# One 256-column product for the next tile's channel mean and this tile's variance, with GpSimd's channel sums moved to the head of its tile

## The chip, the cores and the metric

The kernel runs on one core of a Trainium2 chip. Its time is the device time of one execution in microseconds (us), as the median of several runs. The engines are TensorE (PE, with its weight loads as PEld), VectorE (DVE), ScalarE (ACT), GpSimd (POOL) and SyncE (SP, which issues most of the DMAs). Each works through its own instructions in order, and they meet through semaphores.

## What is computed

One layer of a streaming encoder on 2048 positions of 1024 channels, in float32. A combined projection gives queries, keys, values and the input `u` of a convolution branch. Attention looks at a window of 128 keys and has a sink term per head. The branch is a gated causal convolution with 31 taps, then a layer norm over its 512 channels and swish. Both halves go through a shared output projection, a residual and a layer norm. A gated MLP with a 3-tap convolution and a second residual and layer norm follow. The part that matters here is the norm of the branch:

```python
def layer_norm(x, g, b):
    mu = jnp.mean(xf, axis=-1, keepdims=True)
    var = jnp.mean(jnp.square(xf - mu), axis=-1, keepdims=True)
    y = (xf - mu) * lax.rsqrt(var + LN_EPS)
    return (y * g + b)

def conformer_conv(u, conv_w, conv_b, ln_g, ln_b):
    a, gate = jnp.split(u, 2, axis=-1)
    h = causal_depthwise_conv(a * jax.nn.sigmoid(gate), conv_w, conv_b)
    return jax.nn.silu(layer_norm(h, ln_g, ln_b))
```

## The kernel before, in words

There are four stages: projection with the convolution (until about 317 us of the profiled span), mixing (until about 600 us), up projection and down projection. The change lies in the mixing stage, which works on 16 tiles of 128 positions. It is written out by hand as a software pipeline: in each pass of a loop every engine runs a `body(q, p, c, n, m)` on five tiles at once, where n is the tile whose scores and softmax are made, m = n + 1 the next, and c = n - 1, p = n - 2, q = n - 3 the ones before. A first few passes and the last ones are unrolled around a loop of two tiles per turn (`bodies`). The order of the calls in `body` is the order of the engine's queue.

The branch lies transposed: 512 channels as 4 groups of 128 partitions, 128 positions along the free dimension (`conv_in`). A sum over the channels needs two steps. GpSimd adds the four groups, pairwise and then to one (`sum_conv`, L1428 to L1434, into `conv_sum`; `sum_squares`, L1436 to L1442, into `square_sum`). TensorE then multiplies with a matrix of 1/512 (`ones`), which sums over the partitions and leaves the mean on all of them (`means`, L2373; `variance`, L2391). Mean and variance are written to the same 128 columns of the PSUM bank `aux`, so `means(m)` waits until the variance of n has been used up (`cn_ok`). The next columns hold `ct` and `cr`, steps of the inverse root, and `sink_ps`.

One tile's way through the norm is this. TensorE gives the mean; VectorE subtracts it (`centre`, L2141, into `cc`); ScalarE squares (L1708); GpSimd sums the squares (L1439, L1442); TensorE gives the variance (L2394); ScalarE takes the logarithm and the exponential (`conv_root`, L1723, L1725), which makes an inverse root `cy`; VectorE refines it (`conv_norm`, L2213, L2215, L2217) and scales `cc` (L2220). ScalarE's gate chain (L1731, L1739) and VectorE's swish follow, and they feed the output projection of the next pass (L2413).

The queues around the change, in one pass:

- GpSimd: `cosines(m)` (L1387), `sum_squares(n)`, `sum_conv(m)`, `rotate(m)` (L1415, L1421, L1424, which wait for VectorE's sine products L2135 and L2136), `affine(p)` (L1446, L1448, which wait for VectorE's row norm L2177). The first affine step belongs to tile 0 and runs in the pass of n = 2; the last belongs to tile 12.
- TensorE: `values(c)` (L2470), `scores(n)` (L2386), output products of c (L2413), `turn_values(n)` (L2402), more output products, `variance(n)`, `turn_rows(q)` (L2456), output products of groups 4 and 5, transposes of the probabilities (L2462), output products of groups 6 and 7 (whose end is `y_ps`), `means(m)`.
- VectorE: residual (L2118), gate and attention parts of c, two softmax shifts with `centre(n)` between them, swish, softmax sums (L2205) and reciprocals (L2207), `conv_norm(n)`, row statistics (L2148), sine products, row norm (L117 to L121, L2177).
- ScalarE: casts, exponentials, squares, `conv_root(n)`, probabilities (L1718), copies of the turned rows (L1781), gate inputs, copies of the turned probabilities (L1786), gate chain.

The code of the functions that the diff touches:

Of the kernel before, what the change touches and what calls it, by code (L numbers as in the profile page):

```python
# [793 lines left out]
def phase_rest(nc, block, head, trig_scr, par, con, w_o, ln1_g, ln1_b, h_scr, qkv_scr, conv_scr, h1T_scr, w_tiles, act_scr, w_down, ln_g, ln_b, h1_scr, low_scr, out):  # L794
    ctx, mix, up = ExitStack(), ExitStack(), ExitStack()
    with ctx:
# [32 lines left out]
        conv_pair, square_pair = msb("m_conv_pair", [P, 2, P]), msb("m_square_pair", [P, 2, P])  # L829
        conv_sum, square_sum = msb("m_conv_sum", [P, P]), msb("m_square_sum", [P, P])  # L830
        cy, cln = msb("m_cy", [P, P]), msb("m_cln", [P, P])
# [16 lines left out]
        tps = mps("m_tps", [P, 2 * BLK])  # L848
        mean = var = aux[:, 0:P]
        ct, cr = aux[:, P:2 * P], aux[:, 2 * P:3 * P]  # L850
        sink_ps = aux[:, 3 * P:3 * P + NKV * GROUPS].rearrange("p (g a) -> p g a", g=NKV)
# [268 lines left out]
        def closing(p):  # L1120
            return isinstance(p.t, int) and p.t >= NT - 3

        @block.sync
# [207 lines left out]
        def _(pool):  # L1331
# [96 lines left out]
            def sum_conv(n):  # L1428
                pool.wait_ge(vc_ld[n.slot], n.nth * 32 + 32)
                after(pool, conv_sum_ok, n.t)  # L1430
                nc.gpsimd.tensor_tensor(conv_pair[:, :, :], conv_in[:, n.slot, 0:2, :], conv_in[:, n.slot, 2:4, :], ALU.add).then_inc(conv_pair_ok, 1)
                pool.wait_ge(conv_pair_ok, n.t + 1)
                after(pool, mean_ps, n.t)
                nc.gpsimd.tensor_tensor(conv_sum[:], conv_pair[:, 0, :], conv_pair[:, 1, :], ALU.add).then_inc(conv_sum_ok, 1)  # L1434

            def sum_squares(n):  # L1436
                pool.wait_ge(square_ok, n.t + 1)
                after(pool, square_sum_ok, n.t)
                nc.gpsimd.tensor_tensor(square_pair[:, :, :], squares[:, 0:2, :], squares[:, 2:4, :], ALU.add).then_inc(square_pair_ok, 1)  # L1439
                pool.wait_ge(square_pair_ok, n.t + 1)  # L1440
                after(pool, var_ps, n.t)
                nc.gpsimd.tensor_tensor(square_sum[:], square_pair[:, 0, :], square_pair[:, 1, :], ALU.add).then_inc(square_sum_ok, 1)  # L1442

# [6 lines left out]
            def body(q, p, c, n, m):  # L1450
                if m is not None:
                    cosines(m)
                if n is not None:
                    sum_squares(n)
                if m is not None:
                    sum_conv(m)
                    rotate(m)
                if p is not None and not closing(p):
                    affine(p)
                    if isinstance(p.t, int) and p.t == 0:  # L1460
                        head.clear()
                elif c is not None and p is None:
                    pool.wait_ge(trig_rest_ld, 16 * 8)
                    pool.wait_ge(mrow_ld, 32)
# [441 lines left out]
        def _(dve):  # L1906
# [231 lines left out]
            def centre(n):  # L2138
                dve.wait_ge(mean_ps, n.t + 1)
                after(dve, cact_seq, 4 * n.t - 2)  # L2140
                nc.vector.tensor_tensor(cc[:, :, :], conv_in[:, n.slot, :, :], each(mean, CT), ALU.subtract).then_inc(centre_ok, 1)  # L2141
# [45 lines left out]
            def soft_shift(n, g):  # L2187
# [5 lines left out]
                dve.wait_ge(soft_seq, soft_at(n, g, 1))  # L2193
                dve.wait_ge(mean_ps, n.t + 1)
                nc.vector.scalar_tensor_tensor(out=peak[:, g, :], in0=top[:, g, :], scalar=SCALE, in1=sink_ps[:, g, :], op0=ALU.mult,
# [13 lines left out]
            def conv_norm(n):  # L2209
                seq = Count(cn_seq, dve)  # L2210
                seq.base = n.t * 3
                dve.wait_ge(cy_ok, n.t + 1)
                seq.inc(nc.vector.scalar_tensor_tensor(out=ct, in0=var, scalar=EPS, in1=cy[:], op0=ALU.add, op1=ALU.mult))  # L2213
                seq.wait()
                seq.inc(nc.vector.scalar_tensor_tensor(out=ct, in0=ct, scalar=-0.5, in1=cy[:], op0=ALU.mult, op1=ALU.mult))  # L2215
                seq.wait()
                seq.inc(nc.vector.scalar_tensor_tensor(out=cr, in0=ct, scalar=1.5, in1=cy[:], op0=ALU.add, op1=ALU.mult))  # L2217
                seq.wait()
                assert seq.n == 3
                nc.vector.tensor_tensor(cc[:, :, :], cc[:, :, :], each(cr, CT), ALU.mult).then_inc(cn_ok, 1)  # L2220

# [125 lines left out]
        def _(pe):  # L2347
# [25 lines left out]
            def means(n):  # L2373
                pe.wait_ge(conv_sum_ok, n.t + 1)
                after(pe, cn_ok, n.t)
                nc.tensor.matmul(mean, ones[:], conv_sum[:], start=True, stop=True).then_inc(mean_ps, 1)

# [13 lines left out]
            def variance(n):  # L2391
                pe.wait_ge(square_sum_ok, n.t + 1)
                pe.wait_ge(shift_ok, NKV * n.t + NKV)
                nc.tensor.matmul(var, ones[:], square_sum[:], start=True, stop=True).then_inc(var_ps, 1)  # L2394

# [78 lines left out]
            def body(q, p, c, n, m):  # L2474
# [4 lines left out]
                else:  # L2479
# [8 lines left out]
                    if c is not None:  # L2488
                        project_rest(c)
                if n is not None:  # L2490
                    variance(n)
# [7 lines left out]
                if c is not None:  # L2499
                    project_conv(c, (6, 7))  # L2500
                if m is not None:
                    means(m)

# [365 lines left out]
```

## Time and profile before

| | us |
|---|---|
| median of 3 runs | 1906.34 |
| lowest and highest run | 1905.53, 1906.53 |
| span of the profiled execution | 1901.2 |
| median less span | 5.1 |
| TensorE busy in the span | 1862.5 (98%) |
| VectorE, ScalarE, GpSimd busy | 1537.4, 950.8, 909.4 |

The span runs from the first to the last instruction of one profiled execution; what lies around it in a run is not shown by the profile. Busy times are sums over an engine's instructions, and they say nothing of which engine set the pace. In a timeline a row is: start in us, length in us, engine, line, operation, output <- inputs, shape, count, and in square brackets the idle time of that engine ahead of it with what ended it. One product of float32 operands shows as two matmul records and two weight loads. Ends of matmuls are modelled.

### The profile page before, as it was taken

The numbers are of one execution on the slowest core, as the hardware profiler recorded it, in microseconds if no ns is written. First come the engines' busy times: TensorE is split into PE (matmuls) and PEld (weight loads), VectorE is DVE, ScalarE is ACT, GpSimd is POOL, SyncE is SP. The second block draws the span as 40 slices with busy tenths as digits, with TensorE's granted clock in tenths as the row PEclk, the third lists the DMA queues.
The fourth block names the chain that finished last, engine by engine and source line by source line (L and its number), as shares of the span: only waits on it lengthen the run. The fifth ranks groups of instructions, "written<-read, shape, count | busy, mean of one in ns | idle before, by whom it ended". The sixth has DMA issues, their size and how long they took to land.

```text
span 1901.2 us, 26980 instructions
## 1 busy us (share of the span) xinstructions
PE 1862.5 (98%) x8632; PEld 1527.4 (80%) x8632; DVE 1537.4 (81%) x1938; ACT 950.8 (50%) x1483; POOL 909.4 (48%) x666
## 2 busy tenths in 40 slices
PE   8999999999999899999999999999999999999998
PEld 7888888777777688888888778888888788888886
DVE  8877993799998888988988988878788755676787
ACT  3455662777778545444445444444444532232453
POOL 2169994266675354444545544444443865430000
PEclk9999999999999899999999999999999999999999
DMA  7411123644563433332334332323234654587554
GB/s 280 172 44 44 44 83 122 207 136 143 170 207 111 144 110 124 136 111 105 122 138 170 112 115 101 114 90 109 101 112 145 198 157 140 167 264 246 183 170 144
DMA packets 201828, 265.80 MB, mean 140 GB/s; under 512 B 12320, under 2 KB 131360, under 8 KB 200480
## 3 DMA queue, kind: packets, MB, share of 16 engines
q1 hardware_dynamic: 188096, 229.32, 36.5%
q10 hardware_dynamic: 13664, 35.66, 5.0%
q8 instruction: 32, 0.52, 0.1%
q14 instruction: 36, 0.29, 0.0%
HBM read 177.18 MB, written 87.75 MB: 139 GB/s over the span
## 4 chain that ended last, share of the span: by engine, by line
PE 57%; issue 17%; DVE 11%; POOL 7%; ACT 4%; DMA 2%; SPq 1%; POOLq 0%; DVEq 0%; ACTq 0%
PE d_y L2793 20%; PE u_mm L2364 20%; PE a_mm L250 15%; POOL u_w_sum L1338 1%; ACT m_ce L1739 1%; POOL u_w_sum L1336 1%; PE m_y L2413 1%; POOL u_s L1356 1%; POOL u_s L1359 1%; ACT m_tps L1731 1%; DVE m_stat L2148 1%; POOL u_s L1353 1%; DVE u_w_lo L1909 1%; DVE m_top L2192 1%; DVE m_den L2205 1%
## 5 line engine op out<-in xcount | busy, mean ns | idle before, releaser
L2364 PE MATMUL u_mm<-u_forms,u_w_hi 128*128 128x512 f32 x2464 | 763.1, 391 | 11.0 <-issue 4.6
L2364 PEld LDWEIGHTS u_mm<-u_forms,u_w_hi 128*128 128x128 f32 x2464 | 462.9, 188 | 112.8 <-issue 10.9
L2364 PE MATMUL u_mm<-u_forms,u_w_lo 128*128 128x512 f32 x1232 | 480.8, 390 | 0.0
L2793 PE MATMUL d_y<-d_wd,d_a_hi 128*128 128x512 f32 x1232 | 379.6, 389 | 1.4 <-DVE d_a_lo L1033 1.3
L250 PE MATMUL a_mm<-a_hT,a_w_hi 128*128 128x512 f32 x896 | 278.2, 392 | 1.9 <-DVE a_hT L535 1.9
L2793 PEld LDWEIGHTS d_y<-d_wd,d_a_hi 128*128 128x128 f32 x1232 | 231.0, 188 | 50.2 <-DVE d_a_lo L1033 1.7
L2364 PEld LDWEIGHTS u_mm<-u_forms,u_w_lo 128*128 128x128 f32 x1232 | 232.1, 188 | 48.7
L2793 PE MATMUL d_y<-d_wd,d_a_lo 128*128 128x512 f32 x616 | 239.7, 389 | 0.0
L1949 DVE SCALAR_TENSOR_TENSOR u_y<-u_z,u_taps,u_y 128x1024 f32<-128x1024 f32 x176 | 222.6, 1286 | 10.4 <-DVE u_z L1963 3.1
L1336 POOL TENSOR_TENSOR u_w_sum<-u_w_raw 128x512 f32<-128x512 f32 x44 | 60.2, 1368 | 291.7 <-DMA u_w_raw<-w_up 291.6
L250 PEld LDWEIGHTS a_mm<-a_hT,a_w_hi 128*128 128x128 f32 x896 | 166.7, 188 | 37.5 <-DVE a_hT L535 3.4
L250 PE MATMUL a_mm<-a_hT,a_w_lo 128*128 128x512 f32 x448 | 174.6, 390 | 0.0
L1017 ACT CAST d_a_hi<-d_a_raw 128x1408 fp32r<-128x1408 f32 x56 | 77.0, 1375 | 184.4 <-PE d_y L2793 180.7
L1909 DVE TENSOR_TENSOR u_w_lo<-u_w_raw,u_w_hi 128x512 fp32r<-128x512 f32 x132 | 149.0, 1130 | 21.8 <-ACT u_w_hi L1522 21.7
L1909 DVE TENSOR_TENSOR u_w_lo<-u_w_sum,u_w_hi 128x512 fp32r<-128x512 f32 x176 | 146.9, 840 | 16.8 <-ACT u_w_hi L1522 14.3
L1522 ACT CAST u_w_hi<-u_w_sum 128x512 fp32r<-128x512 f32 x176 | 105.2, 620 | 110.2 <-POOL u_w_sum L1338 45.4
L2413 PE MATMUL m_y<-m_wo,m_mix_hi 128*128 128x512 f32 x512 | 141.9, 402 | 1.5 <-ACT m_mix_hi L1704 1.4
L473 POOL TENSOR_TENSOR a_gb<-a_gb,a_spare 128x512 f32<-128x512 f32 x112 | 130.2, 1212 | 24.3 <-ACT a_spare L392 24.3
L1033 DVE TENSOR_TENSOR d_a_lo<-d_a_raw,d_a_hi 128x1408 fp32r<-128x1408 f32 x56 | 102.7, 1833 | 40.3 <-ACT d_a_hi L1017 39.9
L2793 PEld LDWEIGHTS d_y<-d_wd,d_a_lo 128*128 128x128 f32 x616 | 115.6, 188 | 24.1
L1346 POOL TENSOR_TENSOR u_w_sum<-u_w_raw,u_w_sum 128x512 f32<-128x512 f32 x44 | 63.9, 1452 | 147.2 <-DVE u_w_lo L1909 147.2
L1575 ACT ACTIVATE u_gy<-u_y 128x1024 f32<-128x1024 f32 x44 | 45.2, 1028 | 168.1 <-DVE u_y L1949 168.1
(245 smaller groups left out, 2948.6 us busy)
## 6 DMA issues: line engine op xcount, KB each, us to landing
u_w_raw<-w_up SPq DMA_DIRECT2D x44, 1024.0 KB, 4.9
d_a_raw<-gated_scr SPq DMA_DIRECT2D x56, 704.0 KB, 5.1
gated_scr<-u_s SPq DMA_DIRECT2D x88, 256.0 KB, 2.0
d_wd_raw<-w_down SPq DMA_DIRECT2D x88, 256.0 KB, 5.2
gated_scr<-u_gy SPq DMA_DIRECT2D x44, 256.0 KB, 2.1
a_xs<-x SPq DMA_DIRECT2D x16, 512.0 KB, 5.6
m_h_in<-h_scr SPq DMA_DIRECT2D x16, 512.0 KB, 4.0
h_scr<-m_r SPq DMA_DIRECT2D x16, 512.0 KB, 4.8
```

Source lines behind the costliest of these rows:

```text
L250: last = nc.tensor.matmul(mm[bank][:], w[:, k, :], hT[n][:, part, k, :], start=(k == 0 and w is hi and part == HI_PART), stop=(k == KT - 1 ...
L473: nc.gpsimd.tensor_tensor(p, p, prod[:, i % 2, 0:size], ALU.add).then_inc(part_ok, 1)
L1017: nc.scalar.copy(a_hi[:, u % 2, :, :], a_raw[:, u % 2, :, :]).then_inc(ahi_ok, 1)
L1033: nc.vector.tensor_tensor(a_lo[:, u % 2, :, :], a_raw[:, u % 2, :, :], a_hi[:, u % 2, :, :].bitcast(F32), ALU.subtract).then_inc(alo_ok, 1)
L1336: nc.gpsimd.tensor_tensor(w_sum[:, 0, :, :], a21, raw_of(Q4), ALU.add).then_inc(sum_ok, 1)
L1346: nc.gpsimd.tensor_tensor(w_sum[:, 0, :, :], raw_of(Q2), w_sum[:, 1, :, :], ALU.subtract).then_inc(sum_ok, 1)
L1522: nc.scalar.copy(w_hi[:, s, :, :], left_of(s)).then_inc(whi_ok, 1)
L1909: nc.vector.tensor_tensor(w_lo[:, s, :, :], left_of(s), w_hi[:, s, :, :].bitcast(F32), ALU.subtract).then_inc(wlo_ok, 1)
L1949: v = nc.vector.scalar_tensor_tensor(out=y[:, m, :], in0=z[:, m, k:k + SPAN], scalar=tap(st, m, k), in1=y[:, m, :], op0=ALU.mult, op1=ALU.add)
L2364: last = nc.tensor.matmul(mm[BANK[s]][:], w[:, s, k, :], forms[:, POS[s], part, k, :], start=(s in FRESH and k == 0 and w is w_hi and part ...
L2413: m = nc.tensor.matmul(ym[:, at], a[:, c.slot, k, :], wo_part(part, k)[:, at], start=opens, stop=closes)
L2793: m = nc.tensor.matmul(dy[u % BANKS][:], a[:, u % 2, k, :], wd[:, ph % 2, k, part, :], start=(k == 0 and a is a_hi and part == HI_PART), s ...
```

## The change

The channel sum and the square sum become the two halves of one buffer, `sums`. In the pass of tile n TensorE no longer makes a 128-column product for the variance of n in its middle and another for the mean of n + 1 at its end. It makes one product of 256 columns in the place of the variance, whose first half is the mean of tile n + 1 and whose second half is the variance of tile n. It counts on `var_ps`; `mean_done` says which count stands for the mean of a tile. The means of tiles 0 and 1 and the variances of tiles 0 and 15 are still made by products of their own. For the one product both sums must be there, so GpSimd's `sum_conv(m)` goes from behind `sum_squares(n)` to the head of its pass, ahead of `cosines(m)`, and the product waits for `conv_sum_ok` of m as well. Before `sum_conv` overwrites its half it waits for the product that read it last. Mean and variance have 128 columns each in `aux`, `ct` the third, and the last step of the refinement writes `ct` in place.

```diff
-        conv_sum, square_sum = msb("m_conv_sum", [P, P]), msb("m_square_sum", [P, P])
+        sums = msb("m_sums", [P, 2, P])
+        conv_sum, square_sum = sums[:, 0, :], sums[:, 1, :]
...
-        mean = var = aux[:, 0:P]
-        ct, cr = aux[:, P:2 * P], aux[:, 2 * P:3 * P]
+        mean, var, ct = (aux[:, k * P:(k + 1) * P] for k in range(3))
+        moments = aux[:, 0:2 * P]
...
+        def mean_done(t):
+
+            return (mean_ps, t + 1) if isinstance(t, int) and t < 2 else (var_ps, t)
...
-                after(pool, mean_ps, n.t)
-                nc.gpsimd.tensor_tensor(conv_sum[:], conv_pair[:, 0, :], conv_pair[:, 1, :], ALU.add).then_inc(conv_sum_ok, 1)
+                if not isinstance(n.t, int) or n.t:
+                    pool.wait_ge(*mean_done(n.t - 1))
+                nc.gpsimd.tensor_tensor(conv_sum, conv_pair[:, 0, :], conv_pair[:, 1, :], ALU.add).then_inc(conv_sum_ok, 1)
...
             def body(q, p, c, n, m):
                 if m is not None:
+                    sum_conv(m)
                     cosines(m)
                 if n is not None:
                     sum_squares(n)
                 if m is not None:
-                    sum_conv(m)
                     rotate(m)
...
             def centre(n):
-                dve.wait_ge(mean_ps, n.t + 1)
+                dve.wait_ge(*mean_done(n.t))
...
-                seq.inc(nc.vector.scalar_tensor_tensor(out=cr, in0=ct, scalar=1.5, in1=cy[:], op0=ALU.add, op1=ALU.mult))
+                seq.inc(nc.vector.scalar_tensor_tensor(out=ct, in0=ct, scalar=1.5, in1=cy[:], op0=ALU.add, op1=ALU.mult))
...
+            def variance_and_mean(n, m):
+                pe.wait_ge(conv_sum_ok, m.t + 1)
+                pe.wait_ge(square_sum_ok, n.t + 1)
+                pe.wait_ge(shift_ok, NKV * n.t + NKV)
+                pe.wait_ge(cn_ok, n.t)
+                nc.tensor.matmul(moments, ones[:], sums[:, :, :].rearrange("p s t -> p (s t)"), start=True, stop=True).then_inc(var_ps, 1)
...
-                if n is not None:
+                if m is not None:
+                    variance_and_mean(n, m)
+                elif n is not None:
                     variance(n)
...
-                if m is not None:
-                    means(m)
```

## Rows read from the trace of the kernel before

**Rows 1.** Busy times in the window of the mixing stage's steady part.

```profile
core 0: us, PE busy (x) PEld busy (x) DVE busy (x) ACT busy (x) POOL busy (x), PEclk, DMA share, GB/s
386.00:575.00 189.00, 188.64 (x1094) 149.09 (x1092) 178.24 (x376) 145.25 (x338) 132.04 (x120) 1.00 0.53 164
```

**Rows 2.** Window of one tile's period, same columns.

```profile
433.30:449.47 16.17, 16.13 (x96) 12.72 (x94) 15.27 (x34) 12.51 (x30) 10.90 (x10) 1.00 0.49 145
```

**Rows 3.** GpSimd's groups, 386 to 575 us (count, busy, mean ns, idle before).

```profile
L1431 POOL TENSOR_TENSOR m_conv_pair<-m_conv_in 128x256 f32<-128x256 f32 x12 | 8.8, 731 | 0.0
```

**Rows 4.** Timeline of GpSimd through one tile.

```profile
449.56 2.38 POOL L1446 TENSOR_TENSOR m_r<-m_r,m_g 128x1024 f32<-128x1024 f32 x1 [1.14 <-DVE m_r L2177]
...
454.38 1.57 POOL L1387 TENSOR_TENSOR m_qk_cos<-m_qk_in,m_cos 128x640 f32<-128x640 f32 x1
455.91 0.73 POOL L1439 TENSOR_TENSOR m_square_pair<-m_squares 128x256 f32<-128x256 f32 x1
456.72 0.46 POOL L1442 TENSOR_TENSOR m_square_sum<-m_square_pair 128x128 f32<-128x128 f32 x1
457.15 0.72 POOL L1431 TENSOR_TENSOR m_conv_pair<-m_conv_in 128x256 f32<-128x256 f32 x1
...
458.35 0.24 POOL L1415 COPY m_kr<-m_kr 128x64 f32<-128x64 f32 x1
462.54 0.83 POOL L1421 TENSOR_TENSOR m_kr<-m_qk_cos,m_qk_sin 128x128 f32<-128x128 f32 x1 [3.95 <-DVE m_qk_sin L2135]
```

**Rows 5.** Timelines of TensorE, ScalarE and VectorE around the same tile's variance.

```profile
456.80 0.61 PE L2413 MATMUL m_y<-m_wo,m_mix_lo 128*128 128x512 f32 x2
457.32 0.48 PE L2394 MATMUL m_aux<-m_square_sum,m_ones 128*128 128x128 f32 x2
...
457.31 0.30 PEld L2394 LDWEIGHTS m_aux<-m_square_sum,m_ones 128*128 128x128 f32 x2 [0.32 <-issue]
...
457.84 0.37 ACT L1723 ACTIVATE m_cln<-m_aux,m_eps 128x128 f32<-128x128 f32 x1 [0.61 <-PE m_aux L2394]
458.24 0.31 ACT L1725 ACTIVATE m_cy<-m_cln 128x128 f32<-128x128 f32 x1
...
448.66 0.81 DVE L2177 TENSOR_SCALAR m_r<-m_r,m_mv,m_l 128x1024 f32<-128x1024 f32 x1
...
458.58 0.18 DVE L2207 RECIPROCAL m_inv<-m_den 128x4 f32<-128x4 f32 x1
458.67 0.27 DVE L2213 SCALAR_TENSOR_TENSOR m_aux<-m_aux,m_cy 128x128 f32<-128x128 f32 x1
```

**Rows 6.** TensorE's timeline where a tile starts; then two groups, 386 to 575 us.

```profile
449.01 0.39 PE L2376 MATMUL m_aux<-m_conv_sum,m_ones 128*128 128x128 f32 x2
449.32 1.08 PE L2470 MATMUL m_pv<-m_probT,m_vw 128*64 128x256 f32 x8
...
L2470 PE MATMUL m_pv<-m_probT,m_vw 128*64 128x256 f32 x88 | 11.9, 392 | 0.0
...
L2376 PE MATMUL m_aux<-m_conv_sum,m_ones 128*128 128x128 f32 x22 | 4.3, 274 | 0.0
```

**Rows 7.** GpSimd's timeline for tiles 2 and 15; chain of waits for tile 2.

```profile
371.10 1.56 POOL L1387 TENSOR_TENSOR m_qk_cos<-m_qk_in,m_cos 128x640 f32<-128x640 f32 x1 [2.44 <-PE m_score L2386]
...
584.36 0.74 POOL L1439 TENSOR_TENSOR m_square_pair<-m_squares 128x256 f32<-128x256 f32 x1 [0.60 <-ACT m_squares L1708]
...
368.56 0.22 PE m_aux L2376 x2
...
376.82 0.24 PE m_aux L2394 x2
```

**Rows 8.** Windows where TensorE stood still (columns as in rows 1); chain of waits.

```profile
341.00:345.00 4.00, 2.46 (x26) 1.84 (x26) 3.10 (x3) 3.78 (x6) 0.00 (x0) 1.00 1.00 386
...
636.00:642.00 6.00, 5.58 (x15) 3.89 (x14) 3.23 (x3) 5.21 (x8) 2.90 (x3) 0.61 0.19 57
...
635.35 5.46 PE u_mm L2364 x12
```

**Rows 9.** Chain of waits behind the mixing stage's last probabilities.

```profile
596.72 11.19 PE m_y L2413 x48
```

More of the change, by code:

```diff
@@ L1441, in sum_squares @@
                 after(pool, var_ps, n.t)
-                nc.gpsimd.tensor_tensor(square_sum[:], square_pair[:, 0, :], square_pair[:, 1, :], ALU.add).then_inc(square_sum_ok, 1)
+                nc.gpsimd.tensor_tensor(square_sum, square_pair[:, 0, :], square_pair[:, 1, :], ALU.add).then_inc(square_sum_ok, 1)
             def affine(p):
@@ L2193, in soft_shift @@
                 dve.wait_ge(soft_seq, soft_at(n, g, 1))
-                dve.wait_ge(mean_ps, n.t + 1)
+                dve.wait_ge(*mean_done(n.t))
                 nc.vector.scalar_tensor_tensor(out=peak[:, g, :], in0=top[:, g, :], scalar=SCALE, in1=sink_ps[:, g, :], op0=ALU.mult,
@@ L2216, in conv_norm @@
                 seq.wait()
-                seq.inc(nc.vector.scalar_tensor_tensor(out=cr, in0=ct, scalar=1.5, in1=cy[:], op0=ALU.add, op1=ALU.mult))
+                seq.inc(nc.vector.scalar_tensor_tensor(out=ct, in0=ct, scalar=1.5, in1=cy[:], op0=ALU.add, op1=ALU.mult))
                 seq.wait()
                 assert seq.n == 3
-                nc.vector.tensor_tensor(cc[:, :, :], cc[:, :, :], each(cr, CT), ALU.mult).then_inc(cn_ok, 1)
+                nc.vector.tensor_tensor(cc[:, :, :], cc[:, :, :], each(ct, CT), ALU.mult).then_inc(cn_ok, 1)
             def log_gate(n):
@@ L2375, in means @@
                 after(pe, cn_ok, n.t)
-                nc.tensor.matmul(mean, ones[:], conv_sum[:], start=True, stop=True).then_inc(mean_ps, 1)
+                nc.tensor.matmul(mean, ones[:], conv_sum, start=True, stop=True).then_inc(mean_ps, 1)
             def scores(n):
@@ L2393, in variance @@
                 pe.wait_ge(shift_ok, NKV * n.t + NKV)
-                nc.tensor.matmul(var, ones[:], square_sum[:], start=True, stop=True).then_inc(var_ps, 1)
+                nc.tensor.matmul(var, ones[:], square_sum, start=True, stop=True).then_inc(var_ps, 1)
+            def variance_and_mean(n, m):
[4 more added lines that the diff above has]
+                nc.tensor.matmul(moments, ones[:], sums[:, :, :].rearrange("p s t -> p (s t)"), start=True, stop=True).then_inc(var_ps, 1)
             def turn_values(n):
```

## The prediction

> **What bounds the kernel now.** I read the page first. By its busy times, in the table above, TensorE works for 98% of the span, which invites the reading that any product taken from it is time won. The windows by stage say where the change acts: in the 189 us of the mixing stage's steady part TensorE is busy for 188.64, VectorE for 178.24, GpSimd for 132.04, at full clock [rows 1]. One tile in it takes 16.17 us with TensorE busy for 16.13 and VectorE for 15.27 [rows 2]. Two engines are that full, so a busy share does not decide; the waits within one tile have to be followed.
>
> The timeline of one tile shows a ring. VectorE normalises tile n-2 (L2177) until 448.66 + 0.81 = 449.47. GpSimd starts its affine step (L1446) at 449.56, after waiting 1.14 us for it, and from there issues without a gap: L1446, L1448, the cosines at 454.38, the squares' pair at 455.91, the squares' sum at 456.72, done at 457.18 [rows 3, 4]. TensorE's weight load for the variance starts at 457.31, the product at 457.32, though its weight loads had been idle for 0.32 us: it waited for that sum [rows 5]. ScalarE waits 0.61 us for the product and starts the logarithm at 457.84 and the exponential at 458.24, which ends at 458.55. VectorE's L2213, which needs it, starts at 458.67 [rows 5]. From there VectorE runs down to the next L2177, and that releases GpSimd's next affine step. The ring is closed: its length is the period of 16.17 us [rows 2].
>
> How much play has the ring? Where an engine really waits for another here, the start follows the release by 0.03 to 0.14 us: the logarithm starts 0.04 after the product's end (457.32 + 0.48 = 457.80). L2213 could thus have started at about 458.59. It started at 458.67, right behind VectorE's own reciprocal at 458.58 [rows 5]. So the chain of waits runs along VectorE here, but the ring through GpSimd is only 0.08 us shorter. TensorE has at most about 0.05 us of play at the variance: an output product takes it 0.23 us (11.19 us for 48 [rows 9]), so the last two ahead of the variance, from 456.80 [rows 5], end their turn near 457.26, against 457.32.
>
> **The change part by part.** (a) The channel sums (L1431, L1434) move from behind the squares to ahead of the cosines, so into the ring between affine and squares. Their slot is read from start to start: pair at 457.15, next instruction behind the sum at 458.35, so 1.20 us [rows 4] (the pair alone lasts 0.73 [rows 3]). Before, they ran beside a stretch behind which GpSimd idled for 3.95 us waiting for VectorE's sine products [rows 4], so they cost nothing there; the same 1.20 us ahead of the squares is not covered, because GpSimd has no gap between 449.56 and 457.18. The cosines are delayed as well, but are only read after that idle time. The added wait in the channel sum (for the variance product of the tile before) was fulfilled most of a period earlier: nothing.
>
> (b) The variance is now the second half of a 256-column product. The trace has no such product with 128 rows of output, but has 256-column ones with 64: a record of theirs lasts 392 ns, one of the mean product's 128 columns 274 [rows 6]. Result later by 392 - 274 = 118 ns, say 0.12 us, with the start of the second pass set by the same weight load. Bounds: 0 (the result counts from the issue) to 0.3 (both passes wait in full). I take 0.12, the difference of the two nearest rows.
>
> (c) The product of the mean at the end of each tile (0.31 us, from 449.01 to 449.32 [rows 6]) disappears. That is a true saving of TensorE time, but the product stands behind `y_ps`, and the next one needs ScalarE's transposed probabilities, which come at about the same time. Once the ring is 1.2 us longer TensorE has room, and the saving is worth 0 in the steady part.
>
> (d) The mean now comes a third of a tile or more earlier. The centring on VectorE is not waiting for it in the trace: no idle time stands before it. Worth 0. The separate places of mean, variance and `ct` change only addresses.
>
> (e) Queued behind TensorE's variance wait are the row transposes, the conv products, the probability transposes and, through them, the whole next tile's start. They shift with it. Behind ScalarE's logarithm stand the probabilities and the gate inputs, behind L2213 the rest of VectorE's tile. All of them stand downstream of the same point, so they shift by one amount, not by several.
>
> Sum for one tile: 1.20 + 0.12 - 0.08 (the play) = +1.24 us, so a period of about 17.4 us. How many tiles pay? Those in which the squares follow an affine step and channel sums: n = 3 to 14, twelve, as the twelve records of L1431 in the steady part confirm [rows 3]. For the tiles before, GpSimd waits for scores ahead of the cosines (2.44 us for tile 2 [rows 7]; the two tiles before it wait in the same way), and the channel sums fit into that wait. The last tile has no channel sums ahead, and GpSimd waits 0.60 us for its squares [rows 7]. Twelve times 1.24 is 14.9 us. In tile 2 TensorE itself is the path: the chain runs through the mean product with 0.22 us, which goes, and through the variance product, which grows by 0.12 [rows 7]; -0.1 to -0.3, say -0.2. Nothing behind the stage absorbs the rest: the chain goes from ScalarE into 48 output products of TensorE [rows 9] and on into the next stage, with no load in it that started at a fixed time. Result: +14.7 us on the profiled span of 1901.2, so 1915.9 us of span. The median of the runs, 1906.34, is 5.1 above the span; I add the same, 1906.34 + 14.7 = 1921.0 us.
>
> Bounds: the play taken as 0.14 and (b) as 0 give 1.06 a tile, 12.7 - 0.6 = +12.1 us; (b) as 0.3 and no play give 1.5 a tile, +18 us. So 1918.4 to 1924.4; with 1 us for the spread of medians and another for a second-order loss, 1917 to 1926.
>
> **The rivals.** *Hidden* (time about 1906). The channel sums would be covered after all if something other than the squares' sum released the variance product. For it: the chain of waits never names GpSimd in this stage. Against it: the weight-load idle before L2394 and ScalarE's wait behind it occur in all twelve tiles. At a play of 1.3 us a tile instead of 0.08 the change would cost nothing. Here I also put the case that the diff does less than it seems to.
>
> *Faster* (1902). If TensorE's own stream sets the period, each tile gives back the 0.31 us of the mean product less at most 0.1 for the wider one: fourteen mean products in tiles 2 to 15 go, 14 x 0.31 = 4.3 us, so 1902.0. It decides as long as the squares' sum is there when TensorE gets to the variance at 457.26; it comes at 457.18 now, and 1.20 later after the change. It would take a GpSimd that starts its affine step more than a microsecond earlier, and VectorE, which releases it, has no idle time to give.
>
> *The clock falls* (about 1970). TensorE would now stand still for over 1 us in each tile. The trace shows a stand of 1.5 us between 341 and 345 us with the clock at 1.00 (2.4 GHz), and near 636 us, after stretches in which TensorE was busy for less than half, 0.61, where twelve products took 5.46 us, 0.455 each in place of 0.228 [rows 8]. If half of a tile's 48 output products ran at the lower level (1.2 GHz), that would be 24 x 0.228 = 5.5 us, less 1.2 of idle time, 4.3 a tile, 52 in all: 1921 + 52 = 1973. The steady part would keep TensorE busy for over 90%, which is far from the stretches where it fell. The Trainium skill ("TensorE: Matmul & The Clock Gate", "A second HAM failure mode: psum-queue depth-cycling") describes a kernel in which short idles between groups of matmuls, frequent enough, made the clock go up and down; by that rule the twelve new idles would do it. No row here shows it for idles that short.
>
> **How the numbers follow.** Forecast (GpSimd's sums lengthen the ring) 0.87; hidden 0.05; faster 0.05; clock 0.03. The range 1917 to 1926 holds nearly all of the first. Slower by over 0.2% (3.8 us, about what a measurement of this kernel can tell from none): 0.87 + 0.03 = 0.90. Within: 0.05. Faster: 0.05, though its 4.3 us lie near the edge.
>
> **What would show it.** Right: in the steady part GpSimd goes channel sums, cosines, squares without a gap; the squares' sum ends about 9 us after L1446 starts, not 7.6; TensorE's weight load for the moments stands idle for over 1.2 us before it; VectorE gets idle time before L2213, released by ScalarE's exponential, near 1.2 us; a period near 17.4 us; the clock at 1.00; the stages before and after as long as now. Wrong: a period of 16.2 or less (hidden, faster), L2213 without idle time, or a clock under 1.00 between 386 and 600 us. If the period grows by clearly less than 1.1 us, the play was misread; by more than 1.5, the wide product or a second wait was.

## The result: 19 us slower, and the profile after

| | before | after |
|---|---|---|
| median of the runs of one sitting | 1906.12 (4 runs) | 1925.72 (4 runs) |
| lowest and highest run | 1905.53, 1906.53 | 1924.29, 1927.84 |
| ratio, with its 95% interval | 1 | 1.0099 [1.0082, 1.0116] |
| span of the profiled execution | 1901.2 | 1926.1 |
| TensorE busy in the span | 1862.5 | 1866.5 |
| VectorE, ScalarE, GpSimd busy | 1537.4, 950.8, 909.4 | 1541.1, 950.6, 911.7 |

The median lies 4.7 us above the forecast and just inside its range. The sum behind the forecast was too small, though. Where did the time go? GpSimd's affine step is a mark that comes once per period. These are the rows of its line in both kernels (count, shortest/median/longest in ns, first to last start in us). Lines of the mixing stage stand 5 to 7 further down in the changed kernel, on TensorE up to 13.

```profile
L1446 POOL TENSOR_TENSOR m_r<-m_r,m_g x13: 2374/2382/2392, 384.8 to 578.9; 128x1024 f32<-128x1024 f32 x13
```

```profile
L1452 POOL TENSOR_TENSOR m_r<-m_r,m_g x13: 2374/2383/2387, 388.8 to 602.1; 128x1024 f32<-128x1024 f32 x13
```

Twelve periods take 194.1 us before and 213.3 after: 16.18 and 17.78 each. That is +19.2 of the 24.9 us by which the spans differ. Another 4.0 arise before the first affine step and 1.7 behind the last one.

GpSimd's timeline of one period after, which answers to [rows 4]:

```profile
442.23 2.39 POOL L1452 TENSOR_TENSOR m_r<-m_r,m_g 128x1024 f32<-128x1024 f32 x1 [1.14 <-DVE m_r L2183]
444.69 2.41 POOL L1454 TENSOR_TENSOR m_r<-m_r,m_b 128x1024 f32<-128x1024 f32 x1
447.06 0.74 POOL L1436 TENSOR_TENSOR m_conv_pair<-m_conv_in 128x256 f32<-128x256 f32 x1
447.88 0.46 POOL L1440 TENSOR_TENSOR m_sums<-m_conv_pair 128x128 f32<-128x128 f32 x1
448.29 1.58 POOL L1392 TENSOR_TENSOR m_qk_cos<-m_qk_in,m_cos 128x640 f32<-128x640 f32 x1
449.82 0.74 POOL L1445 TENSOR_TENSOR m_square_pair<-m_squares 128x256 f32<-128x256 f32 x1
450.63 0.45 POOL L1448 TENSOR_TENSOR m_sums<-m_square_pair 128x128 f32<-128x128 f32 x1
451.03 0.23 POOL L1420 COPY m_kr<-m_kr 128x64 f32<-128x64 f32 x1
456.71 0.84 POOL L1426 TENSOR_TENSOR m_kr<-m_qk_cos,m_qk_sin 128x128 f32<-128x128 f32 x1 [5.44 <-DVE m_qk_sin L2141]
459.95 2.38 POOL L1452 TENSOR_TENSOR m_r<-m_r,m_g 128x1024 f32<-128x1024 f32 x1 [1.14 <-DVE m_r L2183]
```

The channel sums stand in the gapless row from affine step to squares' sum, which now ends 8.85 us after the affine step's start (before 457.18 - 449.56 = 7.62). GpSimd's idle time ahead of the rotation grew from 3.95 to 5.44: what was free has moved to where it is of no use.

The other three engines around the same product, in the order TensorE, its weight loads, ScalarE, VectorE, answering to [rows 5]:

```profile
449.34 0.61 PE L2426 MATMUL m_y<-m_wo,m_mix_lo 128*128 128x512 f32 x2
451.43 0.67 PE L2407 MATMUL m_aux<-m_sums,m_ones 128*128 128x256 f32 x2 [1.48 <-POOL m_sums L1448]
...
451.40 0.30 PEld L2407 LDWEIGHTS m_aux<-m_sums,m_ones 128*128 128x128 f32 x2 [1.87 <-issue]
...
452.14 0.37 ACT L1729 ACTIVATE m_cln<-m_aux,m_eps 128x128 f32<-128x128 f32 x1 [2.36 <-PE m_aux L2407]
452.54 0.31 ACT L1731 ACTIVATE m_cy<-m_cln 128x128 f32<-128x128 f32 x1
...
451.13 0.18 DVE L2213 RECIPROCAL m_inv<-m_den 128x4 f32<-128x4 f32 x1
452.88 0.30 DVE L2219 SCALAR_TENSOR_TENSOR m_aux<-m_aux,m_cy 128x128 f32<-128x128 f32 x1 [1.57 <-ACT m_cy L1731]
```

TensorE stands for 1.48 us and VectorE for 1.57, once per tile. The waits from 330 to 620 us (us in all, times, longest) put numbers to both:

```profile
DVE m_aux L2219 <- ACT m_cy L1731: 20.3, 14, 1.6
PE m_aux L2407 <- POOL m_sums L1448: 17.7, 12, 1.5
```

The window of nine periods (columns as in [rows 1]) shows what this makes of the busy shares, at full clock. TensorE, busy for 188.64 of 189 us before, works 146.02 of 160:

```profile
400.00:560.00 160.00, 146.02 (x830) 112.49 (x829) 138.24 (x289) 112.35 (x262) 98.04 (x90) 1.00 0.48 146
```

### The ring, cut into its parts

To compare kernels I cut each period at the same five events and took the mean over 7 to 10 tiles between 400 and 560 us of each timeline. Columns: A, from the affine step's start to the squares' sum's end; B, from there to the logarithm's start, with the handover to TensorE (its sum's end to the product's start) and the product's length beside it; C, from the exponential's end to VectorE's first refining step (L2213, L2219 after); D, from that step to the row norm's start. Logarithm to exponential's end is 0.71 in all kernels, row norm to affine step 0.89.

| kernel | A | handover, product | B | C | D | period |
|---|---|---|---|---|---|---|
| before | 7.63 | 0.13, 0.48 | 0.65 | 0.10 | 6.17 | 16.16 |
| after | 8.90 | 0.34, 0.67 | 1.05 | 0.03 | 6.20 | 17.78 |
| e1, only the order | 8.84 | 0.13, 0.48 | 0.65 | 0.03 | 6.20 | 17.33 |
| e2, cosines behind the squares | 7.38 | 0.34, 0.67 | 1.05 | 0.03 | 6.20 | 16.26 |
| e3, decisive wait last | 8.89 | 0.14, 0.67 | 0.85 | 0.03 | 6.21 | 17.58 |
| e4, mean first, on its own | 8.84 | 0.05, 0.49 | 0.58 | 0.03 | 6.20 | 17.25 |
| e5, e2 and e3 | 7.38 | 0.20, 0.61 | 0.85 | 0.07 | 6.20 | 16.11 |
| g1, before with sines first | 7.11 | 1.07, 0.39 | 1.50 | 0.04 | 5.69 | 15.95 |
| g2, after with sines first | 7.37 | 0.61, 0.60 | 1.24 | 0.03 | 5.70 | 15.95 |

From before to after: A +1.27, B +0.40 (product +0.19, handover +0.21), C -0.07, D +0.03, together +1.63 by the rounded parts and +1.62 by the periods.

### The profile page after: what moved, and what is told of

Same layout as the page of the kernel before. It is cut to its first block, busy times and chain, and to the rows that moved or that the text cites. A ratio compares the mean times of both kernels' runs of the same rounds, so it can differ in the third digit from the quotient of the medians.

```text
span 1926.1 us, 26948 instructions
## 1 busy us (share of the span) xinstructions
PE 1866.5 (97%) x8604; PEld 1525.3 (79%) x8604; DVE 1541.1 (80%) x1938; ACT 950.6 (49%) x1483; POOL 911.7 (47%) x666
## 4 chain that ended last, share of the span: by engine, by line
PE 46%; issue 26%; POOL 14%; DVE 9%; ACT 2%; DMA 2%; SPq 1%; POOLq 0%; DVEq 0%; ACTq 0%
PE d_y L2806 20%; PE a_mm L250 15%; PE u_mm L2370 9%; POOL u_w_sum L1343 2%; POOL u_w_sum L1341 2%; POOL u_s L1361 2%; POOL m_r L1452 1%; POOL u_s L1364 1%; POOL u_s L1358 1%; PE m_y L2426 1%; DVE m_stat L2154 1%; DVE m_l L119 1%; DVE u_w_lo L1915 1%; DVE u_forms L1924 1%; POOL u_s L1367 1%
```

## The experiments

Theory: the period is a ring (affine step, squares' sum, product, root, VectorE's stream, row norm), and each of its parts A to D lengthens it by what it measures. Rivals: the wide product alone costs the time; the order alone does; TensorE's stream, with the mean product taken out, would gain if left alone. The time held against each run is that of the kernel before on the same chip: 1907.25 us (17 runs) for e1 to e4, 1906.69 (29 runs) for the others.

### The same kernel again

The first 4.0 us ahead of the first affine step are in no term of the ring. In the profile after, TensorE stands longer in the first tiles than before, for ScalarE's transposed probabilities. Before first, then after; TensorE's timeline, and a window (columns as in [rows 1]) of each:

```profile
342.54 1.08 PE L2470 MATMUL m_pv<-m_probT,m_vw 128*64 128x256 f32 x8 [1.70 <-ACT m_probT L1786]
343.97 1.16 PE L2386 MATMUL m_score<-m_kr,m_qr 64*128 64x128 f32 x16
...
338.00:352.00 14.00, 12.30 (x69) 9.57 (x68) 8.69 (x11) 10.12 (x16) 2.75 (x2) 1.00 0.89 309
```

```profile
343.68 1.98 PE L2483 MATMUL m_pv<-m_probT,m_vw 128*64 128x256 f32 x8 [3.15 <-ACT m_probT L1792]
346.31 2.08 PE L2392 MATMUL m_score<-m_kr,m_qr 64*128 64x128 f32 x16
...
338.00:352.00 14.00, 10.85 (x50) 7.85 (x50) 7.06 (x9) 7.05 (x11) 2.17 (x4) 0.76 0.92 311
```

After the stand of 3.15 us the granted clock over the window is 0.76, a mix of its two levels (1.2 and 2.4 GHz; before it stands at 1.00, the upper one), and value products and scores take nearly twice their time, 1.98 and 2.08 in place of 1.08 and 1.16. The same program was run again, to see whether that belongs to the change.

> The changed kernel as it is, for a comparison on the same chip. Steady period 17.78 us, time 18 to 21 us over the kernel before. If the scatter of its runs (1924.3 to 1927.8) comes from the opening, where TensorE stood still for 3.2 us before its second group of value products and then ran at a lower clock, a profile whose stand is shorter than about 2 us has its first affine step near 385 us and not 388.8.

Measured: 1926.48 (1923.69 to 1930.37, 4 runs) against 1906.69, ratio 1.0109 [1.0093, 1.0124]. GpSimd's affine step in its profile, and TensorE's stand in the opening:

```profile
L1452 POOL TENSOR_TENSOR m_r<-m_r,m_g x13: 2371/2381/2392, 384.0 to 597.3; 128x1024 f32<-128x1024 f32 x13
...
341.84 1.08 PE L2483 MATMUL m_pv<-m_probT,m_vw 128*64 128x256 f32 x8 [1.17 <-ACT m_probT L1792]
```

The opening is back at 384.0 with a stand of 1.17 us, the span at 1921.9, and the twelve periods take 213.3 us again. So the 4.0 us at the front are scatter of one execution, and the steady part is what the change does. In the profile after, the transfer of `m_wo_raw` that a ScalarE cast ahead of those probabilities waits for landed at 340.57, before at 339.43. That a late landing is the cause is read from these two profiles; it was not tried. An opening can also be late at full clock: in e1 below, TensorE's second group of value products starts at 344.64 (before: 342.54), 2.1 us late behind a stand of 1.86 us, with the clock at 1.00. The first affine step there starts at 388.5, 3.7 us later than before; the rest came behind a lower clock, 0.59 from 368 to 372 us.

### e1: the order alone

```diff
-                    cosines(m)
+                    sum_conv(m)
+                    cosines(m)
                 if n is not None:
                     sum_squares(n)
                 if m is not None:
-                    sum_conv(m)
                     rotate(m)
```

> The kernel before with one edit: GpSimd's channel sums go to the head of its pass; both products stay as they were. Ring theory (the squares' sum, now 1.23 us later, sets the tile): the period grows from 16.17 to 16.17 + 1.23 - 0.09 of play = 17.3 us, in twelve tiles +13.7 us, so about 1920. Rival (the loss comes from the wide product and its waits, the sums are covered): period 16.2, time 1906.

Measured: 1918.88 (6 runs) against 1907.25, 1.0061 [1.0049, 1.0073], period 17.33. Its affine steps, and TensorE's variance:

```profile
L1446 POOL TENSOR_TENSOR m_r<-m_r,m_g x13: 2371/2379/2391, 388.5 to 596.4; 128x1024 f32<-128x1024 f32 x13
...
449.43 0.48 PE L2394 MATMUL m_aux<-m_square_sum,m_ones 128*128 128x128 f32 x2 [1.18 <-POOL m_square_sum L1442]
```

The kernel before, with nothing but GpSimd's order changed, takes 1.17 us more per period (17.33 against 16.16), and TensorE stands 1.18 us for the sum. Handover and product stay at 0.13 and 0.48. This is the largest term, and the rival that the order is hidden falls. It isn't all: 0.45 us per period are missing to after.

### e2: all but the cost of the order

The changed kernel with the cosines behind the squares' sum, so that A holds the channel sums but no longer the cosines:

```diff
                     sum_conv(m)
-                    cosines(m)
                 if n is not None:
                     sum_squares(n)
                 if m is not None:
+                    cosines(m)
                     rotate(m)
```

> The changed kernel with GpSimd's cosines put behind both sums: channel sums, squares, cosines, rotation. Ring theory: 1.53 us leave the stretch between affine step and squares' sum, 17.72 - 1.53 = 16.19 us, unless VectorE's own stream (about 16.15) or the squares, ready 0.6 us after the affine step ends, come later; period 16.15 to 16.3, time 1906 to 1908. Rival (the wide product itself costs, wherever the sums stand): the period stays near 17.7, time 1925.

Measured: 1907.56 (11 runs) against 1907.25, 1.0004 [0.9995, 1.0012], period 16.26.

```profile
L1452 POOL TENSOR_TENSOR m_r<-m_r,m_g x13: 2372/2378/2384, 384.4 to 579.5; 128x1024 f32<-128x1024 f32 x13
```

The wide product and all its waits are in this kernel, and it runs like the one before. The rival that the product itself costs the 19 us falls. B is as long as in after (1.05, +0.40), A is 0.25 shorter than before, and the period follows: 16.26 against 16.16. What the channel sums put into A (1.20), the cosines took out of it (1.53 [rows 4], from 454.38 to 455.91). They had stood in the ring before as well, where nothing needed them.

### e3: the decisive wait last

The 0.21 us of handover were in no part of the prediction. In `variance_and_mean` two more waits stand behind the one for the squares' sum, and in TensorE's queue each is an instruction of its own. The rows of TensorE's sequencer in after (count, shortest/median/longest in ns):

```profile
L2406 PEldq EVENT_SEMAPHORE  x14: 51/51/51, 363.3 to 593.5; - x14
...
L2405 PEldq ALU_OP  x12: 32/32/32, 397.9 to 593.4; - x12
```

```diff
                 pe.wait_ge(conv_sum_ok, m.t + 1)
-                pe.wait_ge(square_sum_ok, n.t + 1)
                 pe.wait_ge(shift_ok, NKV * n.t + NKV)
                 pe.wait_ge(cn_ok, n.t)
+                pe.wait_ge(square_sum_ok, n.t + 1)
```

> The changed kernel with the wait for the squares' sum put last of the four waits ahead of the wide product. In the changed kernel 0.32 us lie between the end of the squares' sum and the weight load, in the kernel before 0.13. Theory (the waits queued behind the decisive one cost that): at least one wait less behind it than in the changed kernel and none left, so 0.32 falls to 0.10 to 0.15, the period by 0.2 to 17.5 us, the time by 2.4 us. Rival (an idle TensorE takes longer to start): 0.32 stays, period 17.72.

Measured: 1924.37 (5 runs) against 1907.25, 1.0089 [1.0076, 1.0102], period 17.58. TensorE around the product, with the sum that releases it:

```profile
447.16 0.45 POOL L1448 TENSOR_TENSOR m_sums<-m_square_pair 128x128 f32<-128x128 f32 x1
...
447.75 0.67 PE L2407 MATMUL m_aux<-m_sums,m_ones 128*128 128x256 f32 x2 [1.23 <-POOL m_sums L1448]
```

The product follows the sum's end by 447.75 - 447.61 = 0.14 us, in the table 0.14 against 0.34, and each period is 0.20 us shorter (210.8 against 213.3 us over the twelve, by the first and last affine start). The intervals of the two ratios overlap, so the times don't tell e3 from after; the table does. The waits that were already fulfilled cost time because they are executed behind the one that decides. The records account for 51 + 51 + 32 = 134 ns of the 0.20; in the kernel before one wait stands behind the decisive one and the handover is 0.13 all the same. How the length comes about in detail stays open.

### e4: the mean first, as a product of its own

```diff
                 pe.wait_ge(conv_sum_ok, m.t + 1)
-                pe.wait_ge(square_sum_ok, n.t + 1)
                 pe.wait_ge(shift_ok, NKV * n.t + NKV)
                 pe.wait_ge(cn_ok, n.t)
-                nc.tensor.matmul(moments, ones[:], sums[:, :, :].rearrange("p s t -> p (s t)"), ...)
+                nc.tensor.matmul(mean, ones[:], conv_sum, start=True, stop=True).then_inc(mean_ps, 1)
+                pe.wait_ge(square_sum_ok, n.t + 1)
+                nc.tensor.matmul(var, ones[:], square_sum, start=True, stop=True).then_inc(var_ps, 1)
```

> The changed kernel with the wide product split in place: TensorE makes the mean product (128 columns) as soon as the channel sum is there, while it waits for the squares, and then a 128-column variance product with one wait of its own. GpSimd's order is that of the change. Ring theory with a wide-product term of 0.19 us and a handover term of 0.2: period 17.72 - 0.4 = 17.3 us, the time 4.7 us under the changed kernel's, about 1920. If only the order of GpSimd counted and neither term existed, 17.7.

Measured: 1918.26 (6 runs) against 1907.25, 1.0060 [1.0048, 1.0073], period 17.25. The sum's end, the mean's product and the variance's:

```profile
445.51 0.46 POOL L1448 TENSOR_TENSOR m_sums<-m_square_pair 128x128 f32<-128x128 f32 x1
...
444.70 0.39 PE L2406 MATMUL m_aux<-m_sums,m_ones 128*128 128x128 f32 x2
446.02 0.49 PE L2408 MATMUL m_aux<-m_sums,m_ones 128*128 128x128 f32 x2 [0.94 <-POOL m_sums L1448]
```

The mean product runs while TensorE would stand anyway (444.70 to 445.09), so it costs nothing. B falls from 1.05 to 0.58, by more than the 0.40 that the wide form had added, because the handover is down to 0.05. Why it is 0.05 here and 0.14 in e3, where no wait stands behind the decisive one either, no run shows. With the order of GpSimd as in after, two products are 0.53 us per period better than one.

### e5: both mends

> The changed kernel with both repairs: cosines behind the sums and the wait for the squares' sum last. Ring theory: the ring is 7.38 + 0.14 + 0.71 (product to logarithm) + 0.71 + 0.03 + 6.20 + 0.89 = 16.06 us, shorter than VectorE's stream of about 16.16, so the second repair pays 0.1 a tile and not 0.2, L2219 (or its like) follows VectorE's reciprocal at once, period 16.16, time that of the kernel before within 0.1%. If the ring were not the limit in the kernel with the cosines last, nothing changes against it (16.26).

Measured: 1907.1 (12 runs) against 1906.69, 0.9999 [0.9987, 1.0011], period 16.11. The 0.20 us that B loses do not arrive in full, 16.26 becoming 16.11. VectorE's timeline says why:

```profile
443.54 0.18 DVE L2213 RECIPROCAL m_inv<-m_den 128x4 f32<-128x4 f32 x1
443.64 0.30 DVE L2219 SCALAR_TENSOR_TENSOR m_aux<-m_aux,m_cy 128x128 f32<-128x128 f32 x1
```

L2219 stands right behind the reciprocal and has no idle time. TensorE has no play left either: the product starts right behind an output product, which is why the handover reads 0.20 and not the 0.14 of e3. VectorE's stream is the bound again, as in the kernel before, and a shorter ring pays no more. This is the play of the prediction, seen from the other side.

### g1 and g2: is there a kernel in which the saved product pays?

If VectorE's stream is what the ring ends on, it must give up time before a TensorE saving can show. In the kernel before, VectorE's row statistics wait for nothing, but its two one-column steps behind them (L117, L119) run while GpSimd adds 512 columns of the rotation (L1424, from 447.12 for 1.29). In g1 three things move: VectorE makes the sine products of m ahead of the row statistics of p, ScalarE the gate inputs ahead of the row root, and GpSimd takes the squares first, then cosines, channel sums and rotation. The products stay two.

```diff
-                if p is not None:
-                    row_stats(p)
                 if m is not None:
                     sines(m)
+                if p is not None:
+                    row_stats(p)
...
+                if n is not None:
+                    gate_inputs(n)
                 if p is not None:
                     row_root(p)
-                if n is not None:
-                    gate_inputs(n)
...
-                if m is not None:
-                    cosines(m)
                 if n is not None:
                     sum_squares(n)
                 if m is not None:
+                    cosines(m)
                     sum_conv(m)
```

> The kernel before (two products, nothing of the change) with three moves that shorten VectorE's stream: VectorE's sine products ahead of the row statistics, so that its two one-column steps (0.42 and 1.22 us beside GpSimd's sums, 0.16 alone) come later than those; ScalarE's gate inputs ahead of the row root; GpSimd's squares ahead of the cosines. VectorE's stream would be some 0.9 us shorter, the ring too. Then TensorE's own stream bounds: added up from the timeline, 16.04 us with at most 0.2 of waits in it. Period 15.85 to 16.05, time 1.5 to 4 us under the kernel before. If VectorE's stretched steps do not shrink: 16.17.

Measured: 1905.3 (12 runs) against 1906.69, 0.9994 [0.9985, 1.0003]: no difference that these runs can tell, and 1.4 us where 1.5 to 4 were expected. The steady period is 15.95, as expected, though the last two of the twelve are 16.88 and 16.74. VectorE's one-column steps, before and in g1:

```profile
446.76 0.42 DVE L117 TENSOR_TENSOR m_l<-m_l 128x1 f32<-128x1 f32 x1
447.21 1.22 DVE L119 SCALAR_TENSOR_TENSOR m_l<-m_l 128x1 f32<-128x1 f32 x1
```

```profile
447.37 0.16 DVE L117 TENSOR_TENSOR m_l<-m_l 128x1 f32<-128x1 f32 x1 [0.89 <-ACT m_l L1755]
447.57 0.16 DVE L119 SCALAR_TENSOR_TENSOR m_l<-m_l 128x1 f32<-128x1 f32 x1
```

L119 takes 1.22 us beside GpSimd's add and 0.16 where GpSimd is idle. It isn't slowed evenly: it ends at 448.43, where the add, started at 447.12, ends at 448.41. Part of the gain is lost to a new wait of 0.89 us for ScalarE's root; D shrinks by 0.5. In the ring the sum now comes more than a microsecond before TensorE takes it (handover 1.07): TensorE's stream is at its bound.

g2 makes the same three moves in the changed kernel, with channel sums, squares, cosines and rotation as GpSimd's order and the decisive wait last.

> The same three moves on the changed kernel, with both repairs (cosines behind the sums, wait for the squares' sum last). Here TensorE bounds, so the product that the change saves is worth its own time: 0.31 us go, the wide product adds 0.1 to 0.2; the period is 0.1 to 0.2 us under that of the same moves on the kernel before, 15.7 to 15.9, and the time 4 to 6 us under the kernel before. If TensorE does not bound there either, the two kernels have the same period.

Measured: 1902.62 (1900.0 to 1903.89, 11 runs) against 1906.69, 0.9975 [0.9966, 0.9984]. It beats both kernels. Its affine steps, and its window to be held against the one of after:

```profile
L1452 POOL TENSOR_TENSOR m_r<-m_r,m_g x13: 2368/2373/2385, 383.4 to 574.5; 128x1024 f32<-128x1024 f32 x13
...
400.00:560.00 160.00, 160.00 (x928) 126.17 (x928) 140.78 (x321) 124.40 (x292) 111.44 (x102) 1.00 0.55 172
```

By the window TensorE is busy for all 160.00 us, and it waits for nobody. The squares' sum is there 0.61 us ahead of the wide product, and ScalarE's copies of the transposed probabilities end 0.56 us ahead of the value products that read them. So TensorE's stream bounds, as expected. Yet the steady period is 15.95, the same as g1's: this expectation was missed. What a product takes of a full queue is read from its start to the start of what follows. TensorE in g1, first the variance, then the mean:

```profile
457.04 0.39 PE L2394 MATMUL m_aux<-m_square_sum,m_ones 128*128 128x128 f32 x2
457.26 1.04 PE L2456 MATMUL m_tps<-m_ident,m_r 128*128 128x128 f32 x8
...
464.74 0.39 PE L2376 MATMUL m_aux<-m_conv_sum,m_ones 128*128 128x128 f32 x2
465.06 1.08 PE L2470 MATMUL m_pv<-m_probT,m_vw 128*64 128x256 f32 x8
```

And in g2, first the wide product, then the place from which the mean product is gone:

```profile
454.88 0.60 PE L2408 MATMUL m_aux<-m_sums,m_ones 128*128 128x256 f32 x2
455.31 1.03 PE L2470 MATMUL m_tps<-m_ident,m_r 128*128 128x128 f32 x8
...
462.33 0.61 PE L2427 MATMUL m_y<-m_wo,m_mix_lo 128*128 128x512 f32 x2
462.87 1.08 PE L2484 MATMUL m_pv<-m_probT,m_vw 128*64 128x256 f32 x8
```

In g1 the two products take 0.22 + 0.32 = 0.54 us. In g2 the wide one takes 0.43, twice the 0.22 of one with half its columns. The mean product's 0.32 held 0.22 for itself and some 0.09 that stand ahead of the value products in any case: in g2 the last two output products ahead of them take 0.54, elsewhere two of them take 0.46. Together 0.43 + 0.08 = 0.51 of the 0.54 are still there; over the 9 or 10 tiles from 402 to 558 us it is 0.52. Making one product of two saves next to nothing of TensorE's time here, because the columns stay the same in number. What the 0.09 ahead of the value products are isn't shown; their first weight load starts together with them in both kernels (462.87 in g2, 465.06 in g1).

Of the gain of 4.1 us (1906.69 - 1902.62), 3.0 lie between first and last affine step: 194.1 us before, 192.7 in g1, 191.1 in g2. The 1.6 between g1 and g2 are for the most part g1's two long periods at the end of the stage (16.88 + 16.74 - 2 x 15.95 = 1.7), which g2 doesn't have. In both, GpSimd has one more add there, of 1024 columns (L1393, L1398 in g2). In g1 it runs from 554.53 to 556.95, and VectorE's sine product L2135, which takes 0.28 in the tile before, takes 1.59 and ends at 557.10. In g2 GpSimd doesn't wait for the squares and gets to this add sooner (8.97 us after its affine step, in g1 9.99); there it ends at 553.98, and the same sine product takes 0.56 and ends at 554.14. That this makes the two periods long is read from the traces and wasn't tried. So the lead of g2 over g1 is one of GpSimd's order, and the wide product has no part in it that the traces show. The other 1.1 us lie outside and within the scatter of opening and end.

## Why the prediction came out as it did

**Right: the ring, and part (a).** Which engines the time runs through was read correctly. The channel sums cost 1.27 us in A (predicted 1.20), and e1 gives 1.17 per period for the order alone (1.20 - 0.08 of play = 1.12). Most of its signs came: GpSimd without a gap, the sum 8.85 us after the affine step (predicted about 9), TensorE's weight loads idle 1.87 us (over 1.2), L2219 idle and released by the exponential (1.57; the size predicted was near 1.2), the clock at 1.00. Two did not: the period is 17.78 and not near 17.4, and in the first profile the time ahead of the first affine step is 4.0 us longer, which the second profile of the same program takes back. The play was 0.07 (predicted 0.08).

**Wrong: part (b) was mis-sized.** It took 0.12 from the difference of single records, 392 - 274 ns [rows 6], and counted it once, for one of the two passes. The product grew by 0.19, from 0.48 to 0.67. By the groups from 400 to 560 us (count, busy, mean ns), before first, then after, both passes lengthen:

```profile
L2394 PE MATMUL m_aux<-m_square_sum,m_ones 128*128 128x128 f32 x20 | 4.8, 324 | 0.1
```

```profile
L2407 PE MATMUL m_aux<-m_sums,m_ones 128*128 128x256 f32 x18 | 6.0, 417 | 13.4 <-POOL m_sums L1448 13.4
```

A record is 417 - 324 = 93 ns longer, and there are two in a product: 0.19. The size of one record was less than assumed, the number of them twice. The bound of 0.3 held.

**Missing: the handover.** 0.21 us more between the sum's end and the product's start. The only added wait that the prediction weighs is GpSimd's, ahead of the channel sum, and that one cost nothing. TensorE's waits ahead of the wide product it didn't look at. Two are new: the one for the channel sums stands ahead of the decisive wait, the one on `cn_ok` behind it, where the kernel before has one wait and the changed kernel two. e3 puts a price of 0.20 on that order.

So the forecast of +1.24 per tile became +1.62, from +0.07 in (a), +0.07 in (b), +0.21 for the handover and +0.03 in D. Twelve times +1.24 is 14.9, twelve times +1.62 is 19.4, against 19.2 measured between first and last affine step. The prediction named the sign of this itself: growth over 1.5 us means that "the wide product or a second wait" was misread; it was both. That the median still lies inside the range is luck. The +1.62 per tile exceeds the upper bound of 1.5, and only the 2 us added for spread and second-order losses cover it, by 0.3 us; a second set of runs of the same kernel has its median at 1926.48. The lower bound also takes off 0.6 us for tile 2, where the text gives 0.3 at most.

**Right for a reason that was only half right: (c).** The saved mean product was worth 0 in the changed kernel, and TensorE has room there once the ring is longer, as said. But it wasn't "a true saving of TensorE time" of 0.31 us either. With TensorE busy throughout, g1 and g2 show that 0.09 of it stay ahead of the value products and that the wide product takes 0.21 more than the narrow one, so about 0.02 is left.

**The others.** (e), one shift and not several, held: the parts of the ring add up to the period. For tile 2's -0.2 no run tells it from the scatter of the opening.

**Misattributed: "5.1 us around the span".** A profiled execution's own time stands 1.7 to 1.9 above its span in every run (1927.84 and 1926.1 here). By that the execution profiled before took some 1903.0 (an estimate, 1901.2 + 1.8) and was simply a quick one; the other 3.3 us were the distance to the median. Added on both sides, this did no harm to the difference, but the comparison of two single spans does contain it: 24.9 us between the spans, 19.6 between the medians.

**The rivals.** *Hidden* falls by e1. *Faster* needed the sum to come a microsecond earlier relative to TensorE; g1 and g2 built that, and the 4.3 us of mean products did not appear even so. Its price was wrong, not only its condition: it took off 0.31 per tile less at most 0.1 for the wider product, and in a full queue the wider product costs 0.21.

*The clock falls* did not happen where it was feared: TensorE stood for 1.4 to 1.5 us ahead of the product in each of twelve tiles, and the clock stayed at 1.00 from 386 to 600 us. The rule of the Trainium skill that was held against this ("TensorE: Matmul & The Clock Gate", "A second HAM failure mode: psum-queue depth-cycling") is not borne out in this part of the kernel. The opening warns against reading this as "a stand of this length is safe". The single stand of 3.15 us was followed by the lower clock, and the stands at the same place in the nine other profiles, 0.90 to 1.86 us long, were not. But a stand of 1.46 us, ahead of the second half of a tile's probability transposes (at 362 to 370 us), is in all ten profiles. Behind it the clock was 0.59 in e1 (368 to 372 us), 0.63 in e5 and 0.62 in g1 (364 to 368), and 1.00 in the other seven, before and after among them. What tells these apart is not shown; the length of the stand alone does not.

## What to carry to other kernels

Before moving work on a helper engine, close the ring through it. Here a step cost its whole start-to-start slot, less the small play, when it landed between the ring's two handovers, and nothing outside them, whatever the engine's busy share; and the same reading shows which step should leave the ring (here the cosines, which nothing in it needed). Where several waits stand ahead of an instruction, put the one that comes last by the trace last in the code. Before counting what a merged product saves, read its slot and those of the two it replaces from start to start in a full queue: here 256 columns took 0.43 us and 128 took 0.22, so the merge saved next to nothing even on an engine that was busy for 100%. And it made the earlier of two results wait for the later: e4, which makes the mean first, is 0.53 us per period better.

## What was not expected of the hardware

- Waits that are already fulfilled are not free when they are queued behind the decisive one: two of them with a register operation, 51, 51 and 32 ns by the sequencer's rows, and the product starts 0.20 us later (0.34 against 0.14).
- A step of VectorE on one column per partition takes 1.22 us beside GpSimd's two-input add of 512 columns and 0.16 alone; the one ahead of it 0.42 and 0.16. The Trainium skill ("GPSIMD Engine Reference", "1. Specifications") says that GpSimd shares its SBUF interfaces with VectorE and contends with it on operations with two SBUF inputs; the trace agrees. The lengths are not a slow-down by some factor: in the kernel before, from 414 to 545 us, each of these steps ends within 0.03 us of the end of GpSimd's running add (L1421 for the first, L1424 for the second). So a step that starts beside such an add costs what is left of the add, however small the step is.
- One product of 256 columns takes twice as long in a full TensorE queue as one of 128 (0.43 against 0.22 us from start to start), so two made into one saved nothing of it.
- One execution of the same program had its opening 4.8 us later than another (388.8 against 384.0), with a stand of TensorE of 3.15 us in place of 1.17 and the lower clock behind it. That is more than the spread of the first four runs after (1924.29 to 1927.84), so a single profile of this kernel can't be held against a median to better than that.
